# Scores of differential attention: 32-row fp32 products in place of 128-row fp32r products of replicated high and low parts

## The reference, cut to what matters

```python
q = _rope(_to_heads(q, 2 * DA_HEADS), pos).reshape(b, DA_HEADS, 2, l, DA_DQK)   # DA_DQK = 32
k = _rope(_to_heads(k, 2 * DA_HEADS), pos).reshape(b, DA_HEADS, 2, l, DA_DQK)
s = jnp.einsum('bhcqd,bhckd->bhcqk', qi, k).astype(jnp.float32) * scale
p = jax.nn.softmax(jnp.where(mask, s, NEG), axis=-1)
w = (p[:, :, 0] - lam * p[:, :, 1]).astype(v.dtype)
o = jnp.einsum('bhqk,bhkv->bhqv', w, v)
```

## Time and profile before

| | before |
|---|---|
| time, median of 3 runs | 3943.01 us (3940.19 to 3950.31) |
| the profiled execution's own time | 3950.02 us |
| its span, first to last instruction | 3948.2 us |
| busy share of the span | PE 84%, PEld 54%, DVE 43%, ACT 20%, POOL 3% |
| mean granted TensorE clock | 0.899 |

### The profile page before, as it was taken

One profiled execution on the slowest core, in us unless ns is written; L12 is line 12 of the kernel. 1 busy time (PEld: TensorE's weight loads), 2 busy tenths in 40 slices (PEclk: granted clock), 3 DMA queues, 4 the chain that ended last, 5 costly groups with the idle time before them and its releaser, 6 DMA issues.

```text
span 3948.2 us, 46980 instructions
## 1 busy us (share of the span) xinstructions
PE 3323.5 (84%) x15268; PEld 2148.3 (54%) x15268; DVE 1687.9 (43%) x2463; ACT 784.7 (20%) x1830; POOL 121.8 (3%) x131
## 2 busy tenths in 40 slices
PE   5999788878796599999769997888787965999994
PEld 3666556656542355555436665566666433555552
DVE  4777524443424122332267775244434241233324
ACT  2222223332211011111122222233322110111111
POOL 2100000000000100000100000000000001000001
PEclk9999997887897799999979998977888977999997
DMA  9400100000100999999820001000001008999996
GB/s 263 137 21 11 38 12 6 6 7 11 43 3 22 355 410 411 410 408 410 313 87 22 21 11 39 12 6 6 7 11 43 3 12 349 414 407 410 409 411 258
DMA packets 141079, 615.53 MB, mean 156 GB/s; under 512 B 13721, under 2 KB 48025, under 8 KB 123033
## 3 DMA queue, kind: packets, MB, share of 16 engines
q1 hardware_dynamic: 104952, 495.89, 31.9%
q0 software_dynamic: 16944, 60.89, 4.8%
q10 hardware_dynamic: 19056, 57.16, 3.9%
HBM read 538.34 MB, written 75.56 MB: 155 GB/s over the span
## 4 chain that ended last, share of the span: by engine, by line
PE 75%; DVE 7%; issue 7%; DMA 5%; ACT 3%; POOL 2%; ACTq 1%; DVEq 1%; SPq 0%; POOLq 0%
PE ps L1080 7%; PE ps L1037 7%; PE ps L1235 6%; PE ps L1336 6%; PE ps L1436 6%; PE ps L1426 6%; PE ps L1395 5%; PE ps L1172 5%; PE ps L1401 5%; PE ps L1453 3%; PE ps L1250 3%; PE ps L1300 3%; DMA arena<-xg 3%; PE ps L1135 3%; PE ps L1160 2%
## 5 line engine op out<-in xcount | busy, mean ns | idle before, releaser
L1172 PE MATMUL ps<-arena 128*64 128x128 f32 (+2 forms) x1440 | 276.3, 331 | 72.4 <-ACT arena L771 40.5
L1080 PE MATMUL ps<-arena 128*128 128x260 f32 x1024 | 294.6, 429 | 34.8 <-DVE rounded L1636 21.1
L1671 DVE TENSOR_REDUCE negmax<-ps 16x1 f32<-16x16 f32 (+8 forms) x216 | 151.5, 705 | 396.1 <-PE ps L1140 395.1
L1037 PE MATMUL ps<-arena 128*128 128x512 f32 (+1 forms) x768 | 259.7, 497 | 5.4 <-DVEq L541 3.2
L1172 PEld LDWEIGHTS ps<-arena 128*64 128x64 f32 (+1 forms) x1440 | 184.1, 163 | 146.5 <-issue 139.7
L1395 PE MATMUL ps<-arena 128*128 128x512 f32 x560 | 254.0, 607 | 2.6 <-ACT arena L959 2.6
L751 ACT ACTIVATE arena<-ps,negmax 16x16 f32<-16x16 f32 (+8 forms) x216 | 151.0, 700 | 519.0 <-DVE negmax L1671 514.8
L1235 PE MATMUL ps<-arena 128*128 128x256 f32 (+1 forms) x1152 | 251.6, 380 | 0.0
L1336 PE MATMUL ps<-arena 128*128 128x512 f32 (+1 forms) x576 | 251.6, 595 | 0.0
L1436 PE MATMUL ps<-arena 128*64 128x256 f32 x2240 | 249.5, 381 | 0.0
L1401 PE MATMUL ps<-arena 128*128 128x256 f32 x1120 | 247.4, 379 | 0.0
(11 more groups left out here) (306 smaller groups left out, 4276.2 us busy)
## 6 DMA issues: line engine op xcount, KB each, us to landing
arena<-w SPq DMA_DIRECT2D x210, 2048.0 KB, 12.9
xg<-arena POOLq DMA_DIRECT2D x51, 512.0 KB, 12.2
arena<-xg ACTq DMA_DIRECT2D x39, 512.0 KB, 10.1
xg<-arena ACTq DMA_DIRECT2D x35, 512.0 KB, 7.6
arena<-w_in SPq DMA_DIRECT2D x16, 1024.0 KB, 5.7
arena<-xg ACTq DMA_DIRECT2D x35, 256.0 KB, 11.2
xg<-arena ACTq DMA_DIRECT2D x70, 128.0 KB, 9.2
arena<-w_in SPq DMA_DIRECT2D x16, 512.0 KB, 4.3
```

The lines of the kernel that those rows point to most:

```text
L1037: mm = pe.matmul(dst[0:hi - lo, a:b], w[:, k, lo:hi], uT[:, k, a:b], start=(k == 0), stop=(k == KD - 1))
L1080: mm = pe.matmul(out, w_qk[b][:, k, :], uT[:, k, lo:hi], start=(k == 0), stop=(k == KD - 1), skip_group_check=True)
L1172: mm = pe.matmul(ps[0:AW, 7, at:at + r], V[0:rows(i), i, n * AW:(n + 1) * AW], WT[0:rows(i), g % 3, m * P:m * P + r], start=(i == 0), stop ...
L1671: v.tensor_reduce(negmax[0:r, at:at + 1], flat[0:r, side:side + wide_], AX.X, ALU.max, negate=True)\
```

## The change

The high and low parts, the matrices `sel` with their load and conversion, and the pieces `c`, `d`, `e`, `f` are gone. DVE's turn (`turn_dve`) writes queries and keys straight into two fp32 operands of 64 partitions, the queries' and keys' channels of map 0 in partitions 0 to 31 and those of map 1 in 32 to 63, and `scores` multiplies 32 rows of them as plain fp32. Masks, maxima, exponentials, turning and outputs are as they were, and so are the FX heads. The plans hold fewer pieces. Waits of `scores` on `t_P` and on the operands now stand as instructions of their own (`wait_alone`) for DA heads. The diff, cut to its core:

```diff
 PLAN_DA = {
     8: [[], [], ["a0.0@2"], ["a0.1@2"], ["a0.2@2"], ["a0.3@2"]],
-    0: [["a1.0@1"], ["a1.1@1"], ["b0@4"], ["a1.2@1"], ["a1.3@1"], ["a2.0@2"]],
-    1: [["c0@4"], ["a2.1@2", "b1@1"], ["d0@4"], ["a2.2@2", "e0@1"], ["f0@4"], ["a2.3@2", "c1@1"]],
-    2: [["o@4"], ["d1@1", "a3.0@2"], ["g@4"], ["e1@1", "a3.1@2"], ["f1@4"], ["a3.2@2"]],
-    3: [["b2@4"], [], ["a3.3@2"], [], ["c2@2"], []],
-    4: [["d2@2"], [], ["e2@2"], [], ["f2@2"], []],
-    5: [["b3@2"], [], [], ["c3@2"], [], ["d3@2"]],
-    6: [[], ["e3@2"], [], ["f3@2"], [], []]}
+    0: [[], [], ["b0@4"], ["a1.0@2"], ["a1.1@2"], ["a1.2@2"]],
+    1: [["a1.3@2"], [], ["b1@4", "a2.0@2"], ["a2.1@2"], ["a2.2@2", "o@1"], ["a2.3@2"]],
+    2: [["g@1"], [], ["b2@4", "a3.0@2"], ["a3.1@2"], ["a3.2@2"], ["a3.3@2"]],
+    3: [[], ["b3@2"], [], [], [], []]}
...
+        turned_sets = [[arena[0:AW, SCRATCH + (4 * b + i) * L:SCRATCH + (4 * b + i + 1) * L] for i in range(2)]
+                       for b in range(2)]
...
-                else:
-                    g = "cdef".index(kind)
-                    if g == 0:
-                        pe.wait_ge(t_parts, ONE + H0 + x + 1)
-                    pe.matmul(out, sel[:, 2 * g, :], xh[(n * PARTS + x) % 2][:, 0:hi - lo], start=True, stop=False)
-                    pe.matmul(out, sel[:, 2 * g + 1, :], xl[(n * PARTS + x) % 2][:, 0:hi - lo], start=False, stop=True)\
-                      .then_inc(t_rep, 1)
...
                     if u >= 2:
-                        pe.wait_ge(t_P, ONE + U0 + u - (0 if j == T - 1 and c == 1 else 1))
-                    pairs_ = [(ops[2 * c], ops[2 * c + 1])] if n < HEADS else \
-                        [(ops[0], ops[1]), (ops[0], ops[2]), (ops[3], DK)]
+                        ready = ONE + U0 + u - (0 if j == T - 1 and c == 1 else 1)
+                        if n < HEADS:
+                            wait_alone(pe, t_P, ready)
+                        else:
+                            pe.wait_ge(t_P, ready)
+                    if n < HEADS:
+                        pairs_ = [tuple(x[DQK * c:DQK * c + DQK] for x in ops)]
+                    else:
+                        pairs_ = [(ops[0], ops[1]), (ops[0], ops[2]), (ops[3], DK)]
...
-            def split_dve(layer, n, piece):
+            def turn_dve(layer, n, piece):
...
+                v.wait_ge(t_rot, ONE + H0 + x + 1)
+                ats.settle()
+                for side in range(2):
+                    half = slice(side * AW, side * AW + AW)
+                    both_ = v.tensor_tensor(ops[side][:, lo:hi], raw[half, 0:hi - lo],
+                                            rot[half, 0:hi - lo], ALU.add)
```

More of the change, by code:

```diff
@@ L231, in build @@
         causal = sb("causal", [P, P])
-        with nc.sbuf_tensor("gamma", [P, D], F32) as gamma:
-            pass
-        gamma_r = sb("gamma_r", [P, D], F32R)
+        gamma = sb("gamma", [P, D])
         gain_hg = sb("gain_hg", [P, DEPTH, HW])
@@ L607, in _ @@
                     sp.dma_start(w_ff, w[:, :, BAND_FF:BAND_FF + HEADS]).then_inc(f_w, 16)
-                    for dst, src in ((sel_read, "c_sel"), (swap, "c_swap"), (cos, "c_cos"), (sin, "c_sin"), (fx_c, "c_fx")):
+                    for dst, src in ((swap, "c_swap"), (cos, "c_cos"), (sin, "c_sin"), (fx_c, "c_fx")):
                         sp.dma_start(dst, A[src]).then_inc(v_t, 16)
@@ L706, in piece_act @@
                 kind, bank = piece[0], int(piece[-1])
-                if kind in "ogbf" or piece[2:4] in (".0", ".1", ".2"):
+                if kind in "ogb" or piece[2:4] in (".0", ".1", ".2"):
                     return
@@ L713, in piece_act @@
                     act.wait_ge(t_proj, ONE + H0 + n * PARTS + x + 1)
-                    act.wait_ge(t_parts, ONE + layer * HEADS * PARTS + n * PARTS + x)
+                    act.wait_ge(t_turned, ONE + layer * HEADS * PARTS + n * PARTS + x)
                     act.activation(raw[:, 0:hi - lo], ps[:, bank, 0:hi - lo], ACT.Copy).then_inc(t_raw, 1)
-                elif kind == "a":
+                else:
                     act.wait_ge(t_proj, ONE + H0 + n * PARTS + x + 1)
@@ L721, in piece_act @@
                        .then_inc(t_qa, 1)
-                else:
-                    g = "cde".index(kind)
-                    act.wait_ge(t_rep, ONE + layer * HEADS * 4 * PARTS + n * 4 * PARTS + 4 * x + g + 1)
-                    act.activation(ops[g][:, lo:hi], ps[:, bank, 0:hi - lo], ACT.Copy).then_inc(t_qa, 1)
             def during_act(layer, at):
@@ L1089, in piece_pe @@
                                          (t_qd, ONE + layer * QD[ALL] + QD[n] + x + 1)]
-                elif kind == "b":
+                else:
                     pe.wait_ge(t_raw, ONE + H0 + x + 1)
@@ L1291, in _ @@
                     pe.wait_ge(v_w, layer * 16 + 16)
-                    wait_alone(pe, v_t, layer * 80 + 80)
-                    wait_alone(pe, s_clean, layer * CLEANS + 8)
+                    wait_alone(pe, v_t, layer * 64 + 64)
+                    wait_alone(pe, s_clean, layer * CLEANS + 7)
                     for bank in range(8):
@@ L1595, in piece_dve @@
                 kind, bank = piece[0], int(piece[-1])
-                if kind in "cde" or piece[2:4] in (".0", ".1", ".2"):
+                if piece[2:4] in (".0", ".1", ".2"):
                     return
@@ L1658, in pieces_dve @@
                 for n, piece in pieces_at(slot - 2):
-                    split_dve(layer, n, piece)
+                    turn_dve(layer, n, piece)
                 for n, piece in pieces_at(slot - 1):
@@ L1761, in attend_dve @@
                     if n == HEADS - 1 and j == 5:
-                        v.wait_ge(t_rep, ONE + (layer + 1) * HEADS * 4 * PARTS)
                         v.wait_ge(t_dec, layer * 2 * HEADS * 16 + 2 * HEADS * 16)
@@ L1912, in _ @@
                 if stop > 2:
-                    wait_alone(v, v_t, layer * 80 + 80)
-                    v.tensor_copy(sel, sel_read).then_inc(s_clean, 1)
+                    wait_alone(v, v_t, layer * 64 + 64)
                     v.tensor_copy(ident_r, ident[:, :]).then_inc(s_clean, 1)
@@ L1919, in _ @@
                     v.memset(rinv_a, 1.0).then_inc(s_clean, 1)
-                    wait_alone(v, s_clean, layer * CLEANS + 8)
+                    wait_alone(v, s_clean, layer * CLEANS + 7)
                     v.wait_ge(f_p, ONE + layer + 1)
@@ L2207, in constants @@
     c["c_sin"] = (np.sin(ang)[n % (DQK // 2)] * scale).astype(f)
-    sel = np.zeros((P, 8, P), f)
-    for g in range(2):
-        for side, low in ((0, (0, 0, 1, 1)), (1, (0, 1, 0, 1))):
-            for m in range(P):
-                sel[side * AW + g * DQK + m % DQK, 2 * (2 * g + side) + low[m // DQK], m] = 1
-    c["c_sel"] = sel
     fx_c = np.zeros((P, 2 + HEADS), f)
```

64 lines of the change are left out of this document (24 added, 40 removed).

## The result

| | before | after |
|---|---|---|
| time, median | 3943.4 us (3940.2 to 3950.3, 4 runs) | 4067.0 us (4063.7 to 4068.0, 4 runs) |
| span of the profiled execution | 3948.2 us | 4064.1 us |
| mean granted TensorE clock | 0.899 | 0.875 |

The changed kernel is slower: the ratio is 1.031, with a 95% interval of 1.0292 to 1.0327. The forecast was 3899 us, in a range of 3855 to 3980. It is wrong in sign and the time lies outside the range. The case that came is the third rival, *the low clock stays*, at a clock lower still than the 0.80 that it was priced with.

The account below looks back on a forecast made before the run. PE was taken as the limit, losing 56.5 us idle and some 44 to low clock in the DA part. Work 178 + 46 + 21 - 15 = 230, plus 17 clock, 20 waits: 267; with value stages -44 us: 3899 us, range 3855 to 3980.

Parts of the forecast that it names:

- the low clock stays: Rival, DA part: 32-row scores do not lift the clock, it stays at 0.80; 307 us, kernel 3980 us; chance 0.13.
- the clock term: DA part: fewer, shorter stops raise the granted clock to 0.93, costing +17 us over full clock where it was +44.
- The prediction's own sign of failure: DA part: prediction fails if granted clock stays near 0.8, or waits ahead of the scores themselves become the largest.
- the tipping point, 0.86: DA part: with 20 us of waits, the clock must be over 0.86 for the change to gain anything.
- Scores, +46 us: DA heads' scores: plain fp32 takes 15.9 us a head instead of 4.4, no credit for idle rows; +46 us per layer.
- Switches, +21 us: DA part: 84 entries into 32-row products per layer at 0.25 us each; +21 us, bounds 0 and 34.
- The `sel` pairs, -15 us: DA part: 48 `sel` pairs at 0.3 us each go; -15 us per layer, bounds 12 and 18.
- Waits, 20 us: DA part: PE waits of 20 us per layer remain of 56.5, those ahead of line 1098 gone; bounds 10 and 35.
- Value stage, -8 us: Value stage, per layer: 16 `sel` pairs (3.8 us) and waits of 3.2 and 1.0 us go; -8 us.
- The stops close nearly altogether: Rival, DA part: clock 1.0 and 15 us of waits left, 245 us; kernel 3856 us; chance 0.15.
- It cancels out: Rival, DA part: switches at upper bound and 7 us more waits, 287 us; kernel 3943 us; chance 0.15.
- the softmax cycle: Rival, DA heads: longer scores lengthen the score, maximum, exponential cycle to 81 us a head; kernel 4013 us; chance 0.07.

Follow-up runs that it names:

- clock_alone: Separate program computing nothing of the reference: PE alone streams plain fp32 products of differing row counts; the 32-row stream fell from clock 1.00 to 0.50.
- pad128: Changed kernel with each map's keys in an operand of 128 rows, zero outside the map's 32; 3884.2 us, ratio to before 0.985.
- pad_0_and_2: Changed kernel with zero-filled 128-row score operands in DA heads 0 and 2 only, 32 rows in heads 1 and 3; 3960.2 us (1.004).
- pad128_switch: `pad128` plus a 32-row, 16-column product adding zero behind each of the 120 score products of a layer's DA part; 4024.3 us (1.020).
- packed: Changed kernel with both maps' 32-row products issued in turn in two row groups in tiles 1 to 7, both masks behind; 3995.3 us (1.014).

## Why the prediction was wrong

**The step that failed is the clock term: a clock of 0.93, taken between head 3's 0.87 and the value stage's 1.00, so "230 / 0.93 = 247" and +17 us over full clock.** The clock was 0.68, and the term measured 105 us in layer 0 (333.4 - 228) and, by 334.0 x (1 - 0.68), 107 in layer 1. The reason given was "Fewer and shorter stops should leave PE more often at 2.4 GHz". The stops did become fewer and shorter, 18 us instead of 56.5, and the clock fell. The value stage's 1.00 and head 3's 0.87 were levels of full-row products, and I carried them to a part in which 137.8 of 333.4 busy us are 32-row products. `clock_alone` shows that such a stream lets the clock fall without any stop, `pad128` and `pad_0_and_2` that filling the rows lifts it in this kernel, and `pad128_switch` (0.87 with 120 entries) and `packed` (0.70 with 48) that the entries, which go with the rows in those two, are at most a smaller part of it. The prediction's own sign of failure, a granted clock near 0.8, was passed on the low side. With 2 x (105 - 17) = +176 us the forecast would have been 4075; the other terms came out some 9 us per layer lower (work 2, waits 2, value stage 2.3, all other stages 2.6), which gives about 4058, against 4067 measured. Most of the last 9 us are the base: the profiled execution of the kernel before lay 6.6 us over its median, that of the changed kernel 1.0 under its.

The rival *the low clock stays* had the mechanism ("if such products do not lift the clock") and the tipping point, 0.86. It got 0.13, since no row showed a 32-row product; that uncertainty asked for more weight and for a high end beyond the clock of before. Pricing it at 0.80 assumed that narrow products would at worst leave the clock alone. At 0.69 it gives 230 / 0.69 + 20 = 353 us, against 351.4 and 352.0.

**Scores, +46 us.** About right: 50 us by both pairs of one-pass and two-pass kernels. No credit for idle rows was right as well: a 32-row record took 34.46 / 40 = 0.86 us at 0.50, twice the 3.43 / 8 = 0.43 us of a 128-row one at 1.00.

**Switches, +21 us.** 16, from two pairs of kernels; 0.19 us an entry on average instead of 0.25, and 0.30 for the one timed alone.

**The `sel` pairs, -15 us.** Not measured by themselves. The whole work is 228 us where the sum had 230; with 50 and 16 in place of 46 and 21 it leaves 178 + 50 + 16 - 228 = 16 for them.

**Waits, 20 us.** 18.0 in layer 0. The composition was off: the swap's 9.0 was put at 3, the outputs' 4.8 at 8, the projections' 2.0 at 4 plus the FX heads' 2.3. In a faster part they come back: 36 us in `pad128`.

**Value stage, -8 us.** -10.3 and -10.2. The reading of the stretch ahead of it was wrong: PE does not multiply there without a stop, it waits 13.05 us for the DMA of `w_in` (13.16 in layer 1). With the load and conversion of `c_sel` gone this wait was 12.58 and 12.50 us. The rest of the 2.3 us in layer 0 is mostly line 1285, whose 32 records took 9.92 us before and 8.47 after; in layer 1 they took 8.73 and 9.17, so that part is no gain of the change.

*The stops close nearly altogether* came true for the stops and not for the clock. *It cancels out* and *the softmax cycle* did not come: PE's idle time ahead of the scores is 0.6 us.

## What to carry to other kernels

A clock seen in the profile belongs to the products that ran there; do not carry it to a change that alters how many rows they fill. Where products have few rows, stand among full-row ones and would take a large share of PE's time, try an operand filled up with zero rows: here it cost PE no time, saved the switches, and took the kernel from 4067 to 3884 us, for a third add per part on DVE and a zeroing once per layer. An idle engine is one reason for a low clock and not the only one, so read the granted clock of the stretch beside its busy time.
